# A state-space scan beside a projection: six homes for the decay matrices, exponentials begun inside the first sweep, a second pass by pairs of heads, and transposes for the states' output

## The reference, cut to what matters

```python
def ssd_mixer(hn, w_in, conv_w, conv_b, dt_bias, a_log, d_skip, norm_g, w_out):
    z, xbc, dt_raw = split(hn @ w_in, ...)            # z: 2048 wide
    xs, bm, cm = split(silu(conv(xbc)), ...)          # 32 heads of 64; 4 groups, state 128
    dt = softplus(dt_raw + dt_bias); log_a = dt * -exp(a_log)
    y = bidir_scan(cm, bm, xs * dt_f, xs * dt_b, log_a_f, log_a_b)   # chunks of 128 tokens
    y = (y + xs * d_skip) * silu(z)
    y = rms_norm_per_group(y) * norm_g                # over the 512 channels of a group
    return y @ w_out

def step(h, inp):                                     # one chunk of one direction
    cs = cumsum(aa); decay = exp(where(mask, cs_j - cs_l, -inf))
    y_intra = ((qq @ kk.T) * decay) @ vv
    y_inter = (qq @ h) * exp(cs)
    h_new = h * exp(cs[-1]) + kk.T @ (vv * exp(cs[-1] - cs))
```

## Time and profile before

| what | value |
|---|---|
| median of 3 runs | 1742.33 us (1742.2 to 1742.42) |
| the profiled execution's own time | 1742.6 us |
| its span, first to last instruction | 1740.9 us |
| mean granted clock of TensorE | 0.998 |
| PE busy | 1709.1 us, 98% of the span |
| DVE busy | 1171.2 us, 67% |
| ACT busy | 790.0 us, 45% |
| POOL busy | 210.1 us, 12% |
| the scan, from the second `z` tile on to the last `norm_sum` | 1044.31 to 1290.71 us, 246.4 us |

### The profile page before, as it was taken

One profiled execution on the slowest core, in us unless ns is written; L12 is line 12 of the kernel. 1 busy time (PEld: TensorE's weight loads), 2 busy tenths in 40 slices (PEclk: granted clock), 3 DMA queues, 4 the chain that ended last, 5 costly groups with the idle time before them and its releaser, 6 DMA issues.

```text
span 1740.9 us, 21624 instructions
## 1 busy us (share of the span) xinstructions
PE 1709.1 (98%) x8558; PEld 1369.1 (79%) x8558; DVE 1171.2 (67%) x1646; ACT 790.0 (45%) x1364; POOL 210.1 (12%) x240
## 2 busy tenths in 40 slices
PE   9999999999999999999999999999989999999998
PEld 6887878776688888888897887776678888888887
DVE  5575774866668887663368996767773788766334
ACT  5565652642245454442244544475552455444221
POOL 1421001442000111110000000221120011111000
PEclk9999999999999999999999999999999999999999
DMA  6211223343222222233313221101113132223332
GB/s 225 98 61 49 73 85 133 96 85 79 67 73 97 98 97 97 97 97 100 96 65 115 85 97 61 37 25 37 37 49 109 62 111 97 98 97 93 98 100 70
DMA packets 45813, 150.04 MB, mean 86 GB/s; under 512 B 5776, under 2 KB 8976, under 8 KB 45584
## 3 DMA queue, kind: packets, MB, share of 16 engines
q1 hardware_dynamic: 41728, 141.89, 24.8%
q0 software_dynamic: 1536, 2.10, 1.1%
q10 hardware_dynamic: 2448, 4.66, 0.8%
HBM read 144.44 MB, written 2.10 MB: 84 GB/s over the span
## 4 chain that ended last, share of the span: by engine, by line
PE 84%; DVE 10%; ACT 4%; issue 1%; DMA 0%; POOL 0%; ACTq 0%; DVEq 0%
PE bank L388 23%; PE bank L390 22%; PE bank L389 22%; PE bank L405 2%; PE bank L407 2%; PE bank L406 2%; DVE w_lo L350 1%; DVE cv L2239 1%; ACT em L2458 1%; PE bank L2346 1%; PE bank L2305 1%; PE bank L985 1%; DVE em L2601 1%; PE bank L998 1%; PE bank L1483 1%
## 5 line engine op out<-in xcount | busy, mean ns | idle before, releaser
L388 PE MATMUL bank<-a_hi,w_hi 128*128 128x512 f32 x1384 | 554.8, 401 | 2.9 <-DVE a_lo L540 2.1
L350 DVE TENSOR_TENSOR w_lo<-raw,w_hi 128x1024 fp32r<-128x1024 f32 (+1 forms) x257 | 327.7, 1281 | 338.1 <-ACT w_hi L343 337.4
L390 PE MATMUL bank<-a_hi,w_lo 128*128 128x512 f32 x1384 | 539.3, 390 | 0.0
L389 PE MATMUL bank<-a_lo,w_hi 128*128 128x512 f32 x1384 | 538.9, 389 | 0.0
L343 ACT ACTIVATE w_hi<-raw 128x1024 fp32r<-128x1024 f32 (+1 forms) x259 | 268.4, 1043 | 305.9 <-DMA raw<-in_w_down 141.4
L388 PEld LDWEIGHTS bank<-a_hi,w_hi 128*128 128x128 f32 x1384 | 259.9, 188 | 76.4 <-issue 19.3
L389 PEld LDWEIGHTS bank<-a_lo,w_hi 128*128 128x128 f32 x1384 | 260.0, 188 | 58.4 <-issue 6.7
L390 PEld LDWEIGHTS bank<-a_hi,w_lo 128*128 128x128 f32 x1384 | 259.8, 188 | 55.0
L1355 ACT ACTIVATE u<-bank,par 128x512 f32<-128x512 f32 x88 | 68.6, 780 | 177.5 <-DVE bank L814 177.5
L1398 POOL TENSOR_TENSOR gv<-u 128x512 f32<-128x512 f32 x44 | 57.4, 1305 | 555.1 <-DVE u L1374 555.1
L388 PE MATMUL bank<-g_hi,w_hi 128*128 128x512 f32 x308 | 119.8, 389 | 0.0
(11 more groups left out here) (403 smaller groups left out, 2526.7 us busy)
## 6 DMA issues: line engine op xcount, KB each, us to landing
raw<-in_w_up SPq DMA_DIRECT2D x88, 512.0 KB, 3.2
raw<-in_w_in SPq DMA_DIRECT2D x50, 512.0 KB, 3.2
raw<-in_w_out SPq DMA_DIRECT2D x32, 512.0 KB, 3.7
raw<-in_w_down SPq DMA_DIRECT2D x32, 512.0 KB, 3.5
raw<-in_w_xbc SPq DMA_DIRECT2D x24, 512.0 KB, 3.2
raw<-in_w_z SPq DMA_DIRECT2D x16, 512.0 KB, 3.2
raw<-in_w_down SPq DMA_DIRECT2D x16, 384.0 KB, 3.1
raw<-in_w_mem_kv SPq DMA_DIRECT2D x4, 512.0 KB, 3.2
```

The costliest lines, as they stand in the source:

```text
L350: nc.vector.tensor_tensor(w_lo[:, q % RING, 0:w], raw[:, q % RING, 0:w], w_hi[:, q % RING, 0:w].bitcast(F32), ALU.subtract).then_inc(lo_do ...
L388: nc.tensor.matmul(out, wh, rhs_hi[:, k, :], start=k == first, stop=False)
L389: nc.tensor.matmul(out, wh, rhs_lo[:, k, :], start=False, stop=False)
L390: return nc.tensor.matmul(out, wl, rhs_hi[:, k, :], start=False, stop=stop)
```

## The change

1. `em` had four homes for decay matrices; there are two more (`matrix_home`, `HOMES` = 6). `decays(n)` for n of 6 and more waits for the `inside` that read the home six steps earlier.
2. `carried` marks its four matmuls as transposes (`is_transpose=True`); operands and places stay.
3. One more `z` tile is made ahead of the scan (three, not two), and every quarter behind it moves up by a tile.
4. `spread` 0 to 7 and `decays` 0 to 5 stand within the sweep: `spread` 2 and 3 before the second `between`, 4 to 7 in a row before the third. `gates(g)` stands after `decays` 3 in every group (before: ahead of `decays` 0, and in the last group after `decays` 3).
5. The second pass goes by pairs of heads: for each of four, one `carried`, filling, two `inside` in a row, with the spreads for the steps two pairs on between them.
6. `turn_x` of the next group is split: its first half stands ahead of the last two `inside` of a group, its second half behind the first quarter of `z` of the next.
7. In the last group the filling is `out3_step` in pairs (`out3_pair(k)`: tile 0 and 1), placed from the sweep on; two steps of tile 2 stand ahead of the last two `inside`, so six and not eight are left for the time before the last `norm_sum`. `low` on DVE and `high` on ACT are placed anew to go with it, `low(8)` to `low(11)` behind the last `evac_y`.

```diff
+    em_more = [at("em4", [P, S], ST + 80), at("em5", [P, S], 97)]
+    matrix_home = [em[:, n, :] for n in range(4)] + [more[:, :] for more in em_more]
...
                 nc.tensor.matmul(bank[2 + i % 2][:, c * P:(c + 1) * P], y12[:, c, i * P:(i + 1) * P], C["ident"],
-                                 start=c == 0, stop=False, skip_group_check=True)
+                                 start=c == 0, stop=False, is_transpose=True, skip_group_check=True)
...
+            part_z(4 * g + 3, 0)
             if g:
-                turn_x(g)
+                turn_x(g, range(2, TT))
...
+            if last:
+                spreads(g, 2, 3)
+                between(g, 1)
+                out3_pair(0)
+                states(g, 2)
+                out3_pair(1)
+            else:
+                part_z(4 * g + 4, 0)
+                spreads(g, 2, 3)
+                part_z(4 * g + 4, 1)
+                between(g, 1)
+                part_z(4 * g + 4, 2)
+                states(g, 2)
+                part_z(4 * g + 4, 3)
+            spreads(g, 4, 5, 6, 7)
             between(g, 2)
             if g:
                 norm_sum(g - 1)
...
+                if i == 0:
+                    if last:
+                        out3_pair(2)
+                    else:
+                        part_z(*first)
+                        part_z(*second)
+                    carried(g, i)
                 else:
...
+                    carried(g, i)
+                    if last:
+                        out3_pair(2 * i + 1)
+                    else:
+                        part_z(*first)
+                    if i < 3:
+                        spreads(g, 4 * i + 4, 4 * i + 5)
...
+                if i == 3 and not last:
+                    begin(g + 1)
+                    turn_x(g + 1, range(2))
+                inside(g, 2 * i)
+                inside(g, 2 * i + 1)
+                if i in (1, 2):
+                    spreads(g, 4 * i + 6, 4 * i + 7)
... (ACT)
-            if n >= 4:
-                act.wait_ge(intra, 8 * g + n // 2 - 1)
+            if n >= HOMES:
+                act.wait_ge(intra, 8 * g + (n - HOMES) // 2 + 1)
... (DVE)
+            weigh_all(g, 0, 1, 2, 3)
+            if last:
+                low(2)
+            weigh_all(g, 4, 5)
+            if g:
+                root_half(g - 1)
+                root_first(g - 1)
+                root_second(g - 1)
+                root_third(g - 1)
+            evac_y(g, 0)
+            weigh_all(g, 6, 7)
+            lo_to(dve, z0 + 4 * g + 6)
+            if last:
+                low(3)
+                low(4)
```

More of the change, by code:

```diff
@@ L2354, in norm_sum, with spreads, out3_pair @@
             nc.tensor.matmul(bank[6][:, :], C["ones"], xbc[:, B_TILE + g, :], start=True, stop=True).then_inc(ysum, 1)
-        for t in range(2):
+        def spreads(g, *steps):
+            for n in steps:
+                spread(g, n)
+        def out3_pair(k):
+            out3_step(pe, 0, k)
+            out3_step(pe, 1, k)
+        for t in range(3):
             for q in range(4):
                 part_z(t, q)
-            turn_x(0, range(2 * t, 2 * t + 2))
+            if t < 2:
+                turn_x(0, range(2 * t, 2 * t + 2))
         tile_gone(pe, "xbc", 23)
@@ L2384, in ssd_pe @@
                 norm_sum(g - 1)
[L2385 to L2391, removed]
-                else:
[L2393 to L2403, removed]
+            for i in range(4):
+                first, second = (4 * g + 5 + i // 2, 2 * (i % 2)), (4 * g + 5 + i // 2, 2 * (i % 2) + 1)
+                if i == 0:
[5 more added lines that the diff above has]
+                    carried(g, i)
+                else:
+                    carried(g, i)
[5 more added lines that the diff above has]
+                        spreads(g, 4 * i + 4, 4 * i + 5)
+                    if not last:
+                        part_z(*second)
+                    elif i < 3:
+                        out3_pair(2 * i + 2)
+                    else:
+                        pe.wait_ge(e_x, STEPS * SG - 1)
+                        out3_step(pe, 2, 0)
+                        out3_step(pe, 2, 1)
+                if i == 3 and not last:
[5 more added lines that the diff above has]
+                    spreads(g, 4 * i + 6, 4 * i + 7)
     def out3_step(pe, t, k):
@@ L2415, in out3_lead_pe @@
     def out3_lead_pe(pe):
-        pe.wait_ge(e_x, STEPS * SG)
-        for k in range(8):
+        for k in range(2, 8):
             out3_step(pe, 2, k)
@@ L2654, in low, with weigh_all @@
             nc.vector.tensor_tensor(y_lo[:, k, :], xbc[:, k, :], y_hi[:, k, :].bitcast(F32), ALU.subtract).then_inc(ylo, 1)
-        take_z(0)
-        take_z(1)
-        for g in range(SG):
-            if g:
-                masks(g)
-                tailed(g, 0)
-            else:
-                tailed(0, 0)
+        def weigh_all(g, *steps):
+            for n in steps:
+                weigh(g, n)
+        for t in range(3):
+            take_z(t)
+        for g in range(SG):
+            last = g == SG - 1
+            tailed(g, 0)
+            if g == 0:
@@ new lines, in ssd_dve @@
+            weigh_all(g, 8, 9)
+            evac_y(g, 1)
+            if last:
+                low(5)
+            weigh_all(g, 10, 11)
+            lo_to(dve, z0 + 4 * g + 7)
+            if last:
+                low(6)
+            if g:
+                normed_y(g - 1, 2)
+                normed_y(g - 1, 3)
+            if not last:
+                take_z(4 * g + 5)
+            weigh_all(g, 12, 13)
+            evac_y(g, 2)
+            if last:
+                low(7)
+                lo_to(dve, z0 + 4 * g + 8)
@@ L2696, in ssd_dve @@
+            weigh_all(g, 14, 15)
+            if not last:
+                take_z(4 * g + 6)
+                masks(g + 1)
             evac_y(g, 3)
-            if g + 1 < SG:
-                take_z(4 * g + 5)
-        low(11)
+        for k in range(8, 12):
+            low(k)
         lo_to(dve, z0 + 4 * SG + 6)
```

135 lines of the change are left out of this document (59 added, 76 removed).

## The result

The changed kernel takes 1746.14 us (median of 20 runs, 1742.39 to 1750.84) against 1742.09 us (20 runs, 1741.7 to 1742.81) of the kernel before: a ratio of 1.0022, 95% interval 1.0015 to 1.0029. It is 4 us slower, where 1740.5 us was forecast, and it lies 1.1 us above the range. Its runs spread over 8.5 us, those of before over 1.1. Its profiled execution took 1746.29 us.

The account below looks back on a forecast made before the run. PE, busy for 1709.1 of 1740.9 us, was taken as the bound. The scan falls from 246.4 to 241.6 us (-4.8), the clock costs 3.0, leaving -1.8: 1740.8 profiled, 1740.5 us as median; range 1736.5 to 1745.

Parts of the forecast that it names:

- Part 5, the clock: Last group: idle time lowers PE's granted clock; two low stretches at 1.5 us each, 3.0 us lost, bounds 0 and 5.1.
- the three long waits: Waits of PE in the last group, forecast at 3.0, 3.3 and 4.6 us.
- Part 1, transposes: Sixteen `carried` as transposes cost 0.49 instead of 0.98 us: 7.8 us less, minus some 0.1 at each of twelve places.
- Part 2, second pass: Groups 0 to 2: middle groups 53.85 us instead of 57.63, with a new wait of 2.1 us at the four spreads.
- Part 3: Ahead of the scan: four quarters of `z` move ahead of group 0, so 8.47 becomes 13.95 us; no gain by itself.
- Part 4, the last group: Output steps wait for `low`: last group 68.0 us, like for like 4.4 us slower than 63.6.
- The clock mostly holds: Faster rival: none or one low stretch in the changed kernel, giving 1737.5, up to 1739 us; chance 0.30.
- The four spreads cost the clock: Slower rival: a low stretch follows the four spreads, groups 0 to 2 lose 1.5 us each, total 1745; chance 0.11.
- at the matmul's pace: Slower rival: transposes that open a sum leave `carried` at 0.98 us, total 1747; chance 0.05.
- at a quarter: Faster rival: transposes bring `carried` to 0.25 us, total 1737.6; chance 0.02.
- DVE held up the middle groups: Same-time rival: busy DVE makes a wait of 1 us in each middle group, total 1742 to 1743; chance 0.10.

Follow-up runs that it names:

- Experiment 1: Changed kernel with unread matmuls put into PE's waits of the last group, none taken away: 1739.67 us, 0.9984 of the kernel before.
- experiment 3: Changed kernel with `carried` as ordinary matmuls, no `is_transpose`: 1748.99 us; and the kernel before with `is_transpose` as its only edit: 1740.94 us.
- experiment 6: Changed kernel with last group reordered and spreads 6 and 7 behind `norm_sum`, then without `is_transpose`: 1729.0 us, against 1723.75 with it.
- Experiment 4: Changed kernel with spreads 6 and 7 moved behind the third `between` instead of ahead of it: 1734.71 us, 0.9960 of the kernel before.

## Why the prediction was wrong

**The failed step is Part 5, the clock.** I counted one low stretch behind two of the three long waits, 3.0 us in all. The profiled execution has 20.5 us at half clock, six times 3.4. All three of the long waits have one behind them (1248.6, 1258.9, 1289.6), the last of double length, and two more come where I had none: behind the waits of 1.1, 1.0 and 0.5 that end at 1241.4, and behind one of 1.89 that ends at 1271.6. The price of a stretch I had nearly right. One stretch is 3.4 / 1744 x 0.5 = 0.001 of the mean clock, and a straight line through the 20 runs of the changed kernel (0.991 with 1750.84 us, 0.997 with 1742.39) gives 1.26 us for 0.001; I had 1.5. So the count of stretches failed, six for two, and not their price. Experiment 1 filled the waits and left the order: -6.5 us.

The account, against the 1740.8 forecast for the profiled execution and the 1746.29 measured: ahead of the scan -0.3; groups 0 to 2 and the tile ahead -1.4 (172.2 instead of 173.65); the last group at full clock +1.6 (69.6 in experiment 1 instead of 68.0); the clock +5.0 (75.5 - 69.6 in the group and 2.1 behind it, 8.0 instead of 3.0); outside the span +0.5. The sum is +5.4 of 5.5.

- **Part 1, transposes.** 0.53 in front of `inside`, where I had 0.49, and 0.36 to 0.41 in front of `z` and output steps, where the matmuls took 0.81 to 0.91; 0.45 less each, against the 0.49 and some 0.39 that I had. The Trainium skill, "TensorE: Matmul & The Clock Gate", "Terms", says four times faster for float32; the rows show 1.8 to 2.3 times. What a middle group gains by them, 1.04 in experiment 3 and 1.5 in experiment 6, is less than four times 0.45, since the wait for `zt` behind the third takes part of it back. I had counted them at 6.6 us in all; in the changed kernel they are worth 2.9.
- **Part 2, second pass.** The length is right, 53.56 and 53.53 for 53.85, but partly by luck, as two errors cancel: the wait of the spreads has 1.53 and not 2.1, and the wait for `zt`, 0.5 a group, I had missed. Experiment 4 shows that both go when the spreads are set apart, and more than that: this one line cost 11.4 us.
- **Part 3.** 13.93 for 13.95.
- **Part 4, the last group.** Waits of 1.54, 1.11, 1.53, 2.88, 4.35, 0.36, 1.89, 0.36 and 4.34, where I had 1.6, 1.3, 2.0, 3.0, 3.3, 0.3, 1.8, 0.3 and 4.6. Two are off. The 1.53 is that of the spreads, as above. The other is 4.35: ahead of `low(3)` stand two `weigh`, for which I had 1.2 (2 x 0.60). DVE's timeline there:

```profile
1254.52 0.75 DVE L2651 SCALAR_TENSOR_TENSOR xbc<-xbc,par,bank 128x512 f32<-128x512 f32 x1 [1.56 <-PE bank L2349]
1255.18 2.35 DVE L2646 TENSOR_TENSOR em<-em,gmat 128x512 f32<-128x512 f32 x2
```

and POOL's at the same time:

```profile
1255.35 1.64 POOL L2578 TENSOR_TENSOR xbc<-xbc,zt 128x512 f32<-128x512 f32 x1 [27.38 <-DVE xbc L2651]
```

They take 2.35 us beside POOL's product, against 1.29 for two in the earlier trace rows, where it is not running. In group 1 of the changed kernel two `weigh` take 2.39 at 1143.93, beside the same product, and 1.28 at 1149.31, without it. So an estimated 1.1 of the last group's 1.6 is this. The Trainium skill, "GPSIMD Engine Reference", "Specifications", says that GpSimd shares its SBUF interfaces with VectorE and contends with operations of two SBUF inputs; `weigh` is one, and this row agrees.
- **The rivals.** "The clock mostly holds" (1737.5) is what the layout does once its waits are filled, in experiment 1. "The four spreads cost the clock" named a true place: in the profiled executions of experiment 1 and of experiment 3 without transposes (from 1135.5 on) such a stretch stands behind those of group 1. But in the changed kernel's profiled execution all six lie in or behind the last group. Transposes were neither at the matmul's pace nor at a quarter, and DVE held up the middle groups by the 0.5 for `zt` alone.

A rival that I had not named is that transposes do not count as work for the clock. The Trainium skill says so in the same page's "Part 4: PE-mode transpose". It is not settled here. In the changed kernel the runs without them have a mean clock of 0.9950 (5 runs) against 0.9944 (20 runs), and in experiment 6 the two are alike (0.9978 and 0.9977). In the kernel before, the transposes went with 0.9974 against 0.9983. All of it is small against the six stretches that made the miss.

What stays open: 0.4 us lie outside the first and last instruction more than before (2.1 and 1.7) in every kernel with the changed order and in none with the order before, the one with transposes alone included. Nothing here says why.

## What to carry to other kernels

Where the matrix engine is the bound and its clock is granted by activity, price a wait twice: its own length, and the slower work behind it. So lay out an order by where its waits cluster and not by their sum; 18 us of waits in one group of heads cost 8.0 us beyond their length. When a long wait can't be removed, independent work put into it can pay even if nobody needs the result. A piece in a chain that hardly waits is worth most of its duration (5.25 of 7.2 us in experiment 6), and the same piece ahead of waits is worth a fraction (1.3 in the kernel before), so remove waits first and count the cheaper operation after.

## What the runs showed of the hardware that was not expected

- The clock is no fixed function of the order: twenty executions of one program had mean clocks of 0.991 to 0.997 and times 8.5 us apart. The four spreads of group 1 left 1.00 in the changed kernel and 0.51 in experiment 1, with PE busy for 1.89 and 1.88 of 3.4 us before. The row of the changed kernel:

```profile
1131.56:1134.98 3.42, 1.89 (x6) 0.86 (x5) 0.00 (x0) 2.18 (x8) 0.00 (x0) 1.00 0.46 153
1134.98:1138.39 3.41, 3.41 (x12) 2.08 (x11) 2.93 (x5) 1.35 (x3) 0.00 (x0) 1.00 0.02 5
```

- Several waits of 0.5 to 1.1 us close together brought the clock down as one of 4.3 did. The Trainium skill, "TensorE: Matmul & The Clock Gate", "A second HAM failure mode: psum-queue depth-cycling", tells of such short idle times between bursts; the rows from 1238.39 to 1245.21 us agree.
- A float32 transpose of 128x128 that opens a sum costs about what one standing alone costs: 0.53 for four, against 0.49 in the earlier trace rows, and 0.36 where a 128x512 matmul follows.
